# Later modulation columns: summed in the ticks of the attention instead of in the gated recurrence

## Chip, core and metric

The kernel runs on one core of a Trainium2 chip. The metric is device time in microseconds (us) of one execution, smaller is better. Three runs of the kernel before have a median of 3149.4 us.

## What is computed

One layer of a decoder trunk on 1024 tokens of width 1024, in float32. What matters for the change is where the modulation comes from and where it is used:

```
mod = silu(c) @ W_ada + b_ada -> sh1, sc1, g1, sh2, sc2, g2     # 6 x 1024 columns
h   = rms_norm(x) * (1 + sc1) + sh1
proj = h @ w_in                      # columns of three branches and of their gates
o_a = (rg_lru(conv4(lru_x)) * gelu(lru_y)) @ w_lru_o     # A: gated recurrence, width 1280
o_b = rwkv7_time_mix(...) @ w_rw_o                       # B: pairs of heads
o_c = sliding_window_attention(q, k, v) @ w_att_o        # C: 16 heads, 4 key heads, window 128
x   = x + g1 * ((gate_a * o_a + gate_b * o_b + gate_c * o_c) @ w_out)
h2  = rms_norm(x) * (1 + sc2) + sh2
x   = x + g2 * swiglu(h2)
```

The first 2048 columns of `mod` (sh1, sc1) are needed for h. The other 4096, here called the later columns, are first needed after the branches are merged.

## The kernel before, in words

Activations stand transposed: 128 channels on the partitions by 1024 tokens. Every dense product is made with operands split in a high and a low part, in three passes (`three_passes`, L246). One weight **block** is 1024 x 128 (512 KB): SP loads it into one of two slots of `w_raw` (`load_block`, L228; for the attention's keys and values in two halves, L546), POOL splits it into `w_hi` and `w_lo` (`split_block`, L236 and L238), and PE waits for the split before the block's first matmul and then runs 48 matmuls. A load waits until the block before the last is split, a split until the dense product before the last is done. Each engine executes its own list in order, and so does SP: a transfer behind a waiting one is not issued.

The stages stand one after the other: start, B in 8 turns, A in 2 turns, C, the merges of A, C and B, `w_out`, the feed-forward part.

**Gated recurrence (A), 2 turns of 5 column groups j.** PE's order in a turn is x0 x1 y0 x2 y1 x3 y2 x4 y3 y4 (`LRU_ORDER`), and after each y_j the eight matmuls of the gates (`lru_gates`, L866 and L867). They need the halo rows that ACT copies (L1204, L1206) once DVE has made the convolution of x_(j+1) (`conv`, one L1646 and three L1649), which needs ACT's copy of x_(j+1) out of PSUM (L1199). After the gates ACT takes sigmoids, exponentials and the root (L1211 to L1217), DVE makes the recurrence of group j (`recur`, L1668 to L1681), and ACT then waits for it and issues the store of `ya` to `y_a` (L1219), before it goes on. DVE's order is conv(j+1), sums of the later columns, recur(j).

**Later columns.** A product of a vector with a matrix: DVE multiplies weights with `c` on the partitions and adds up over 8 row tiles, and a matmul with a column of ones (L879) adds over the partitions. In a turn SP loads 16 blocks of 1024 rows by 128 columns in four lots of four (L538), each after the product two before it; DVE makes eight steps of 128x128 for each (`ada_sum`, L1421 and L1424), four blocks in each of the groups j = 0 to 3; PE sums four blocks at a time before y_1 to y_4, and waits for DVE there.

**Attention (C), 35 ticks.** A tick is a unit of two query blocks for a pair of heads; 8 ticks make a group with one key head. In tick t PE makes the scores of unit t (L952), transposes the probabilities of unit t - 2 (L965) and weighs the values of unit t - 3 (L977). Between these it puts 8 of the 48 steps of the next group's projection, in the first six ticks of a group: block 3 in ticks 0 and 1, block 4 in 2 and 3, block 5 in 4 and 5, block 6 in 8 and 9 and so on to block 11 in 20 and 21. Blocks 3, 6 and 9 hold keys and values. Ticks 6, 7, 14, 15 and all from 22 have no projection. DVE in tick t: `peaks(t)` (L1745 to L1754), `divide(t-1)` (L1760 to L1764), and in ticks 2, 3 and 6 of a group squares and norms of the next group (`k_sums` L1714 and L1717, `k_norm` L1722 and L1724, `q_rsqrt` L1731). SP's list there holds the blocks alone, then the first tiles of `y_a` (L561).

## Time and profile before

| | us |
|---|---|
| median of 3 runs | 3149.4 (3149.35 to 3154.89) |
| profiled execution: its own time | 3150.59 |
| profiled execution: span | 3148.8 |
| gated recurrence, 20 dense blocks | about 1289 to 1619 |
| attention's ticks | about 1671 to 1935 |

The profile's times are of one execution and count from the start of the span. Its page gives each engine's busy time and shares; the timeline lists instructions of one engine in order of time; the chain of waits is followed back from the last instruction. A row `x8` merges eight records; one float32 matmul that is no part of a split product leaves two records.

### The profile page before, as it was taken

To read this page: it belongs to the slowest core of one execution; us is meant where nothing else is said; L and a number is where in the kernel's file an instruction comes from. 1 tells how busy PE (TensorE), PEld (TensorE's weight loads), DVE (VectorE), ACT (ScalarE), POOL (GpSimd) and SP (SyncE) were. 2 spreads that over 40 slices of the span, in tenths; PEclk is the share of its full clock that TensorE was granted. 3 is DMA by queue.
4 is the path that set the end of the run, shared out by engine and by line. 5 is a ranking of instruction groups with operands and counts; after the bars stand their busy time and mean duration, and the time that the engine had idled before them with its cause. 6 is when DMAs were issued, how large, how long until landed. Compare 5 with 4: busy or idle time off the path is not lost.

```text
span 3148.8 us, 61688 instructions
## 1 busy us (share of the span) xinstructions
PE 2926.4 (93%) x25715; PEld 2385.0 (76%) x25715; DVE 1458.6 (46%) x1801; ACT 706.7 (22%) x1004; POOL 724.0 (23%) x454
## 2 busy tenths in 40 slices
PE   1899999999999999999979988989897999999998
PEld 1687878787888888776757766777685888888886
DVE  6555454555454554675744655445523222222222
ACT  1222121212121221244435664001202000000001
POOL 0212020203021111132312101333231333333331
PEclk7999999999999999999989998999897999999999
DMA  5111111102010110233421102333410111111111
GB/s 179 49 44 35 37 42 31 54 19 70 23 50 29 44 36 29 78 109 88 124 64 38 44 14 83 115 122 128 134 54 27 47 47 53 47 47 47 53 47 67
DMA packets 247066, 192.75 MB, mean 61 GB/s; under 512 B 21729, under 2 KB 225083, under 8 KB 246843
## 3 DMA queue, kind: packets, MB, share of 16 engines
q1 hardware_dynamic: 239136, 163.02, 17.5%
q10 hardware_dynamic: 7707, 26.34, 2.1%
q8 instruction: 191, 3.13, 0.4%
q14 instruction: 32, 0.26, 0.0%
HBM read 158.91 MB, written 30.41 MB: 60 GB/s over the span
## 4 chain that ended last, share of the span: by engine, by line
PE 84%; DVE 8%; ACT 4%; issue 3%; DMA 1%; ACTq 0%; DVEq 0%; POOL 0%; SPq 0%; POOLq 0%
PE ps L246 59%; PE ps L772 2%; PE ps L786 2%; PE ps L783 2%; PE ps L750 2%; DVE arena L1424 2%; PE ps L835 1%; PE ps L866 1%; PE ps L867 1%; PE ps L952 1%; PE ps L977 1%; PE ps L965 1%; DVE arena L1649 1%; PE ps L720 1%; ACT arena L1275 1%
## 5 line engine op out<-in xcount | busy, mean ns | idle before, releaser
L246 PE MATMUL ps<-x_hi,w_hi 128*128 128x512 f32 (+1 forms) x2576 | 839.5, 401 | 49.9 <-DVE x_lo L1850 17.7
L246 PE MATMUL ps<-x_lo,w_hi 128*128 128x512 f32 (+1 forms) x2576 | 821.8, 395 | 0.0
L246 PE MATMUL ps<-x_hi,w_lo 128*128 128x512 f32 (+1 forms) x2576 | 820.0, 394 | 0.0
L236 POOL CAST w_hi<-w_raw 128x1024 fp32r<-128x1024 f32 (+2 forms) x221 | 224.1, 1014 | 2365.4 <-PE ps L246 1629.4
L246 PEld LDWEIGHTS ps<-x_hi,w_hi 128*128 128x128 f32 (+1 forms) x2576 | 485.1, 191 | 189.6 <-issue 66.1
L246 PEld LDWEIGHTS ps<-x_hi,w_lo 128*128 128x128 f32 (+1 forms) x2576 | 489.6, 190 | 106.7
L246 PEld LDWEIGHTS ps<-x_lo,w_hi 128*128 128x128 f32 (+1 forms) x2576 | 490.9, 191 | 104.4
L238 POOL TENSOR_TENSOR w_lo<-w_raw,w_hi 128x1024 fp32r<-128x1024 f32 (+2 forms) x221 | 484.2, 2191 | 17.7
L1856 DVE TENSOR_TENSOR arena<-ps,arena 128x1024 f32<-128x1024 f32 x22 | 26.9, 1225 | 396.3 <-PE ps L246 396.3
L1873 DVE SCALAR_TENSOR_TENSOR arena<-ps,mod,arena 128x1024 f32<-128x1024 f32 x88 | 113.0, 1284 | 129.1 <-PE ps L246 129.1
L1591 DVE COPY_PREDICATED arena<-hid_lo,ps 128x256 f32<-128x256 int32 x144 | 72.0, 500 | 139.8 <-PE ps L783 90.4
L1424 DVE SCALAR_TENSOR_TENSOR arena<-arena,mod 128x128 f32<-128x128 f32 (+1 forms) x280 | 129.0, 461 | 10.0
L1374 ACT ACTIVATE hid_hi<-arena 128x1024 fp32r<-128x1024 f32 x22 | 23.4, 1062 | 450.7 <-PE ps L246 316.9
L246 PE MATMUL ps<-hid_hi,w_hi 128*128 128x512 f32 x352 | 109.1, 391 | 4.8 <-DVE hid_lo L1861 4.8
L246 PE MATMUL ps<-hid_lo,w_hi 128*128 128x512 f32 x352 | 108.8, 390 | 0.0
L246 PE MATMUL ps<-hid_hi,w_lo 128*128 128x512 f32 x352 | 108.8, 390 | 0.0
L1275 ACT ACTIVATE arena<-arena 128x256 f32<-128x256 f32 x128 | 75.4, 591 | 84.4 <-DVE arena L1754 84.4
L786 PE MATMUL ps<-arena 64*64 64x64 f32 x2560 | 89.4, 218 | 0.0
L1504 DVE TENSOR_TENSOR arena<-arena 128x1024 f32<-128x1024 f32 (+1 forms) x27 | 42.9, 1588 | 98.3 <-ACT arena L1120 97.3
L772 PE MATMUL ps<-arena 64*64 64x64 f32 x2560 | 84.5, 218 | 0.7
L786 PEld LDWEIGHTS ps<-arena 64*64 64x64 f32 x2560 | 83.2, 135 | 0.2 <-issue 0.2
L772 PEld LDWEIGHTS ps<-arena 64*64 64x64 f32 x2560 | 80.2, 135 | 1.7 <-issue 1.6
(263 smaller groups left out, 3541.5 us busy)
## 6 DMA issues: line engine op xcount, KB each, us to landing
w_raw<-in_w_in SPq DMA_DIRECT2D x78, 512.0 KB, 3.9
w_raw<-in_w_ffn_in SPq DMA_DIRECT2D x44, 512.0 KB, 3.8
arena<-in_w_ada SPq DMA_DIRECT2D x32, 512.0 KB, 3.8
gates_sig<-arena ACTq DMA_DIRECT2D x24, 512.0 KB, 2.6
arena<-gates_sig SPq DMA_DIRECT2D x24, 512.0 KB, 3.4
w_raw<-in_w_ffn_out SPq DMA_DIRECT2D x22, 512.0 KB, 3.5
arena<-in_x SPq DMA_DIRECT2D x16, 512.0 KB, 5.1
arena<-in_w_ada SPq DMA_DIRECT2D x8, 1024.0 KB, 12.0
```

Source lines behind the costliest of these rows:

```text
L236: nc.gpsimd.tensor_copy(hi, raw).then_inc(s_whi, 1)
L238: nc.gpsimd.tensor_tensor(lo, raw, hi.bitcast(F32), ALU.subtract).then_inc(s_wsplit, 1)
L246: ins = nc.tensor.matmul(dst[h], wp, xp[h], start=first and m == 0, stop=last and m == 2)
L750: ins = mm(dst, src[hp, c * CHUNK:(c + 1) * CHUNK], ar[hp, c, :, :], start=True, stop=True)
L772: ins = mm(bank(B, 2, hp)[:, c % BATCH, :], am[hp, c, AM_BA, :], xx[hp, 0, c, :], start=True, stop=True)
L783: ins = mm(bank(B, 0, hp)[:, c % BATCH, :], xx[hp, 1, c, :], y1[hp, c, :], start=True, stop=True)
L786: ins = mm(bank(B, 1, hp)[:, c % BATCH, :], y1[hp, c, :], xx[hp, 1, c, :], start=True, stop=True)
L1275: fn(sc[:, h, nn, :], sc[:, h, nn, :], ACT.Exp, bias=sm[:, SM_NEG, h, nn:nn + 1], scale=rq[:, gg % 2, t, n0 + nn, h:h + 1], accum_out=sm[: ...
L1424: ins = v.scalar_tensor_tensor(acc, w[:, k, :], c_k, acc, ALU.mult, ALU.add)
L1504: v.tensor_tensor(dst, x0, x1, ALU.subtract).then_inc(v_mix, 1)
L1591: v.copy_predicated(blocks_of(xx[:, o, batch(B), :], lv, o), level_mask(lv, o), blocks_of(bank(B, o), lv, o)).then_inc(v_xu, 1)
L1873: v.scalar_tensor_tensor(r, ps[:, 4 + 2 * (m % 2):6 + 2 * (m % 2), :], mod[:, MOD_G2 + m:MOD_G2 + m + 1], r, ALU.mult, ALU.add).then_inc(m ...
```

## The change

The 4096 later columns are taken 1024 columns by 128 rows a step: 32 steps, eight to each set of 1024 columns, 24 ticks. A step is one DVE instruction of 128x1024 (`later_ada`). The loads go through two free slots (`yraw`), each after the step two before it, and stand in SP's list between the blocks of the attention. PE sums each set with eight matmuls in ticks 6, 12, 18 and 24. One addition after the last tick puts the columns into `mod`, and PE waits for it before the merges. In the gated recurrence the loads, steps and sums go away; the store of group j is issued behind ACT's copy of x_(j+2), the last two behind the gelu and at the end. The load of the first tiles of `y_a` waits for all 32 steps.

```diff
         halo = lr["halo"].rearrange("p (s n) -> p s n", s=2)
...
         l_halo = made_by("act", "lru_halo_ready")
-        ada_acc1 = lr["acc"].rearrange("p (s m) -> p s m", s=4)
...
-        ADA_G = (LRU_G - 1) * ADA_PHASE
         s_adb = [sem(f"later_ada_weights_loaded_{k}") for k in range(2)]
...
-        l_pe, l_ada = made_by("pe", "lru_gates_done", "ada_sums_taken")
+        l_pe, t_ada = made_by("pe", "lru_gates_done", "later_ada_sums_taken")
         l_cv, l_sq, l_u, l_out, l_z, gw_zero = made_by(
...
-        mg = carve([("x2", KT * T), ("mix", KT * T), ("gt", 2 * T), ("t", 2 * T), ("pad", 1536), ("yraw", 2 * T)])
+        mg = carve([("x2", KT * T), ("mix", KT * T), ("gt", 2 * T), ("t", 2 * T), ("pad", 1536), ("yraw", 2 * T), ("more", T)])
...
         yraw = mg["yraw"].rearrange("p (s n) -> p s n", s=2)
+        ADA_TICKS = ALL - UNITS
+        ada_acc1 = mg["more"]
         gtl = mg["gt"].rearrange("p (s n) -> p s n", s=2)
...
                         load_gate_weights(g, j)
-                    if c in (4, 6, 8, 9):
-                        first = ADA_PHASE * (4, 6, 8, 9).index(c)
-                        for n in range(first, first + ADA_PHASE):
-                            sp.wait_ge(ada_acc, upto(g * ADA_G + (ADA0 + n - 1)))
-                            wait_alone(sp)
-                            sp.dma_start(ada_w1[:, n % 2, :, :], cols(w_ada, ADA0 * 256 + n * P + g * (ADA_G * P), P)).then_inc(s_adb[n % 2], 16)
+            def load_ada(first, last):
+                for n in range(first, last):
+                    sp.wait_ge(ada_acc, upto(ADA0 + n - 1))
+                    sp.dma_start(yraw[:, n % 2, :], w_ada[n % KT * P:(n % KT + 1) * P, 1024 * (n // KT + 2):1024 * (n // KT + 3)]).then_inc(s_adb[n % 2], 16)
...
                     sp.dma_start(dst[:, :, s, :], src).then_inc(s_w[b.slot] if s else s_kfirst, 16)
+                if gg > 0:
+                    load_ada(11 * (gg - 1), 11 * (gg - 1) + 3)
                 for t in range(2):
                     load_block(sp, Block("att", 3 * gg + 1 + t), cols(w_in, COL_Q + 256 * gg + P * t, P), P)
+                    if gg > 0:
+                        first = 11 * (gg - 1) + 3 * t + 3
+                        load_ada(first, min(first + 3 + 2 * t, ADA1))
                 if gg == 0:
...
                         sp.wait_ge(m_lo, upto(n - 1))
+                        sp.wait_ge(ada_acc, upto(ADA0 + ADA1))
                         sp.dma_start(yraw[:, n % 2, :], y[row0 + k * P:row0 + (k + 1) * P, :]).then_inc(s_y[n % 2], 16)
...
                 pe.wait_ge(v_post, upto(PAIRS * POST))
-                pe.wait_ge(ada_out, upto(g * (LRU_G - 1) + (ADA0 + j)))
                 n = 2 * 16 * len(PIECES_OF[j])
...
                         pe.wait_ge(a_gate, upto(PAIRS * 3))
-                    if kind == "y" and j > 0:
-                        pe.wait_ge(ada_acc, upto(g * ADA_G + (ADA0 + ADA_PHASE * j)))
-                        pe.wait_ge(l_sa, upto(g * (2 * LRU_G) + 2 * j))
-                        for q in range(ADA_PHASE):
-                            ins = mm(ps[:, 4, q:q + 1], ada_acc1[:, q, :], ones[:, 0:1], start=True, stop=True)
-                        ins.then_inc(l_ada, 1)
                     dense(pe, Block("lru", c, g))
...
                 ins.then_inc(t_o, 1)
+            def ada_sums(u):
+                pe.wait_ge(ada_acc, upto(ADA0 + KT * (u + 1)))
+                for n in range(8):
+                    ins = mm(ps[:, BANK_O, 256 + 8 * u + n:257 + 8 * u + n], ada_acc1[:, n * P:(n + 1) * P], ones[:, 0:1], start=True, stop=True)
+                ins.then_inc(t_ada, 1)
...
                     project(nx, fill + 3, fill + 6)
+                if 0 < tick <= ADA_TICKS and tick % 6 == 0:
+                    pe.wait_ge(t_oc, upto(tick - 3))
+                    ada_sums(tick // 6 - 1)
                 if 0 <= tick - 3 < ALL:
...
             pe.wait_ge(t_cp, upto(6 * GROUPS))
+            pe.wait_ge(ada_out, upto(ADA0 + 1))
             for g, (nm, kts, *_) in enumerate(BR):
...
             with act.Fori(0, TURNS["lru"]) as g:
+                def store_y(j):
+                    act.wait_ge(l_out, upto(g * LRU_G + (j + 1)))
+                    act.dma_start(y_a[bass.ds(g * (LRU_G * P) + j * P, P), :], lr["ya"]).then_inc(s_ya, 16)
                 for c, (kind, j) in enumerate(LRU_ORDER):
...
                         fn(halves(lr["xp"][:, 3:T + 3]), pair_of(blk.slot), ACT.Copy).then_inc(l_ev, 1)
+                        if j >= 2:
+                            store_y(j - 2)
                         continue
...
                     fn(halves(lr["gy"]), pair_of(blk.slot), ACT.Gelu_apprx_tanh).then_inc(l_ev, 1)
+                    if j == LRU_G - 1:
+                        store_y(j - 1)
                     act.wait_ge(l_pe, upto(g * LRU_G + (j + 1)))
...
                     fn(lr["a2"], lr["a2"], ACT.Sqrt, scale=-1.0, bias=one_b).then_inc(l_rt, 1)
-                    act.wait_ge(l_out, upto(g * LRU_G + (j + 1)))
-                    act.dma_start(y_a[bass.ds(g * (LRU_G * P) + j * P, P), :], lr["ya"]).then_inc(s_ya, 16)
+                    if j == LRU_G - 1:
+                        store_y(j)
...
-            def later_ada(g, j):
-                dve.wait_ge(l_ada, upto(g * (LRU_G - 1) + j))
-                for q in range(ADA_PHASE):
-                    n = ADA_PHASE * j + q
-                    dve.wait_ge(s_adb[n % 2], g * (16 * ADA_G // 2) + 16 * (n // 2 + 1))
-                    ada_sum(ada_acc1[:, q, :], ada_w1[:, n % 2, :, :], g * ((KT - 1) * ADA_G) + (KT - 1) * (ADA0 + n))
-            def later_ada_add(g, j):
-                dve.wait_ge(l_ada, upto(g * (LRU_G - 1) + (j + 1)))
-                cols4 = mod[:, bass.ds(g * ADA_G + (2 * ADA0 + ADA_PHASE * j), ADA_PHASE)]
-                v.tensor_tensor(cols4, ps[:, 4, 0:ADA_PHASE], cols4, ALU.add).then_inc(ada_out, 1)
+            def later_ada(n):
+                c_k = mod[:, 48 + n % KT:49 + n % KT]
+                dve.wait_ge(s_adb[n % 2], 16 * (n // 2 + 1))
+                if n % KT == 0:
+                    dve.wait_ge(t_ada, upto(n // KT))
+                    ins = v.tensor_scalar(ada_acc1, yraw[:, n % 2, :], c_k, None, ALU.mult)
+                else:
+                    dve.wait_ge(ada_acc, upto(ADA0 + n))
+                    ins = v.scalar_tensor_tensor(ada_acc1, yraw[:, n % 2, :], c_k, ada_acc1, ALU.mult, ALU.add)
+                ins.then_inc(ada_acc, 1)
...
                         conv(g, j + 1)
-                    if j > 0:
-                        later_ada_add(g, j - 1)
-                    if j + 1 < LRU_G:
-                        later_ada(g, j)
                     recur(g, j)
...
                     q_rsqrt(nx)
+                if tick < ADA_TICKS:
+                    for n in range(ADA1 * tick // ADA_TICKS, ADA1 * (tick + 1) // ADA_TICKS):
+                        later_ada(n)
                 if tick - 1 in Y_TICKS:
...
+            dve.wait_ge(t_ada, upto(ADA1 // KT))
+            dve.wait_ge(t_oc, upto(ALL))
+            later = mod[:, 2 * ADA0:2 * ADA0 + ADA1]
+            v.tensor_tensor(later, ps[:, BANK_O, 256:256 + ADA1], later, ALU.add).then_inc(ada_out, 1)
+            dve.wait_ge(ada_out, upto(ADA0 + 1))
             v.tensor_scalar(mod[:, MOD_SC2:MOD_SC2 + 8], mod[:, MOD_SC2:MOD_SC2 + 8], 1.0, None, ALU.add).then_inc(ada_fix, 1)
```

On **SP**, in the attention, the list of transfers (L546, after it L545, are halves of the keys' and values' block, L228 the others, L537 the later columns' weights). Before:

```order
L552 DMA arena<-in_consts 128x512
L546 DMA w_raw<-in_w_in 128x8x64 x2
L228 DMA w_raw<-in_w_in 128x8x128 x2
L546 DMA w_raw<-in_w_in 128x8x64 x2
L228 DMA w_raw<-in_w_in 128x8x128 x2
```

And with the change, the same stretch up to block 9:

```order
L556 DMA arena<-in_consts 128x512
L545 DMA w_raw<-in_w_in 128x8x64 x2
L537 DMA arena<-in_w_ada 128x1024 x3
L228 DMA w_raw<-in_w_in 128x8x128
L537 DMA arena<-in_w_ada 128x1024 x3
L228 DMA w_raw<-in_w_in 128x8x128
L537 DMA arena<-in_w_ada 128x1024 x5
L545 DMA w_raw<-in_w_in 128x8x64 x2
L537 DMA arena<-in_w_ada 128x1024 x3
L228 DMA w_raw<-in_w_in 128x8x128
L537 DMA arena<-in_w_ada 128x1024 x3
L228 DMA w_raw<-in_w_in 128x8x128
```

Every block from block 4 on stands behind a lot of three or five loads of the later columns.

On **ACT**, in the gated recurrence, around the copy of an x block. Before:

```order
L1217 ACTIVATE arena<-arena,bias_t 128x1024
L1219 ISA
L1219 DMA y_a<-arena 128x1024
L1196 REGISTER_ALU
L1199 ACTIVATE arena<-ps 128x1024
```

With the change (L1234 is L1217, L1212 is L1199, L1203 is L1219):

```order
L1234 ACTIVATE arena<-arena,bias_t 128x1024
L1209 REGISTER_ALU
L1212 ACTIVATE arena<-ps 128x1024
L1203 ISA
L1203 DMA y_a<-arena 128x1024
```

The copy now stands ahead of the store and of the wait for it.

On **DVE**, in tick 11 and the start of tick 12, with the change (L1735 is L1724, L1756 is L1745):

```order
L1733 RECIPROCAL arena<-arena 128x8
L1735 TENSOR_TENSOR arena<-arena 128x1024
L1677 SCALAR_TENSOR_TENSOR arena<-arena,mod 128x1024 x2
L1756 TENSOR_TENSOR arena<-ps,arena 128x1024
L1758 TENSOR_REDUCE arena<-arena 128x4
```

Before, L1745 followed L1724 at once; now two steps of the later columns stand between.

## Rows read from the trace of the kernel before


**Rows 1.** The page, busy time of each engine.

```profile
PE 2926.4 (93%) x25715; PEld 2385.0 (76%) x25715; DVE 1458.6 (46%) x1801; ACT 706.7 (22%) x1004; POOL 724.0 (23%) x454
```

**Rows 2.** Timeline of PE, recurrence: start us, us, line, form, [idle before <-releaser].

```profile
1329.02 1.12 PE L867 MATMUL ps<-arena 64*128 64x512 f32 x2
1330.07 0.72 PE L246 MATMUL ps<-x_hi,w_hi 128*128 128x512 f32 x2
...
1341.11 0.95 PE L879 MATMUL ps<-keep,arena 128*128 128x1 f32 x8
...
1354.57 1.12 PE L866 MATMUL ps<-arena 128*128 128x512 f32 x2 [1.48 <-ACT arena L1206]
...
1386.12 1.13 PE L866 MATMUL ps<-arena 128*128 128x512 f32 x2 [1.67 <-ACT arena L1206]
```

**Rows 3.** Timeline of PE, last y block of both turns.

```profile
1429.39 1.86 PE L879 MATMUL ps<-keep,arena 128*128 128x1 f32 x8 [4.58 <-DVE arena L1424]
...
1444.12 1.02 PE L866 MATMUL ps<-arena 128*128 128x512 f32 x2
...
1594.98 1.87 PE L879 MATMUL ps<-keep,arena 128*128 128x1 f32 x8 [6.61 <-DVE arena L1424]
...
1610.50 1.02 PE L866 MATMUL ps<-arena 128*128 128x512 f32 x2
```

**Rows 4.** Timeline of ACT, same stretch as rows 2.

```profile
1338.58 1.15 ACT L1217 ACTIVATE arena<-arena,bias_t 128x1024 f32<-128x1024 f32 x1
...
1345.92 1.03 ACT L1199 ACTIVATE arena<-ps 128x1024 f32<-128x1024 f32 x1 [6.19 <-DVE arena L1681]
...
1353.46 1.05 ACT L1206 ACTIVATE arena<-arena 64x1024 f32<-64x1024 f32 x1
```

**Rows 5.** Timeline of DVE, same stretch.

```profile
1343.53 1.69 DVE L1681 TENSOR_TENSOR arena<-arena 128x1024 f32<-128x1024 f32 x1 [0.22 <-DVE arena L1677]
1347.16 0.88 DVE L1646 TENSOR_SCALAR arena<-arena,lru_par 128x1024 f32<-128x1024 f32 x1 [1.93 <-ACT arena L1199]
...
1351.06 1.28 DVE L1649 SCALAR_TENSOR_TENSOR arena<-arena,lru_par 128x1024 f32<-128x1024 f32 x1 [0.15 <-DVE arena L1649]
```

**Rows 6.** Timeline of SP in attention: transfers issued.

```profile
1690.72 17.94 SPq L228 DMA_DIRECT2D w_raw<-in_w_in  x2
```

**Rows 7.** Tile w_raw, 1600 to 1800 us: ns min/median/max.

```profile
L236 POOL CAST w_hi<-w_raw x10: 1036/1036/1041, 1610.8 to 1791.6; 128x1024 fp32r<-128x1024 f32 x10
L238 POOL TENSOR_TENSOR w_lo<-w_raw,w_hi x10: 2342/2394/3247, 1611.9 to 1792.7; 128x1024 fp32r<-128x1024 f32 x10
```

**Rows 8.** DMA issues, 1313 to 1321 us: KB each, median us to landing.

```profile
arena<-in_w_ada SPq DMA_DIRECT2D x2, 512.0 KB, 4.6
```

**Rows 9.** Timeline of DVE in ticks 2, 6, 11 and 17.

```profile
1695.51 0.69 DVE L1717 TENSOR_REDUCE arena<-arena 128x8 f32<-128x512 f32 x1
...
1732.28 0.35 DVE L1731 RECIPROCAL arena<-arena 128x32 f32<-128x32 f32 x1 [4.28 <-ACT arena L1266]
...
1773.37 1.72 DVE L1724 TENSOR_TENSOR arena<-arena 128x1024 f32<-128x1024 f32 x1
...
1818.72 1.22 DVE L1764 TENSOR_TENSOR arena<-arena 128x1024 f32<-128x1024 f32 x1
```

**Rows 10.** The chain of waits in attention: start us, us, what.

```profile
1703.58 1.06 PE ps L952 x8
1704.64 2.27 PE ps L246 x9
...
1739.37 1.07 PE ps L965 x8
...
1772.70 1.06 PE ps L952 x8
...
1823.57 1.06 PE ps L952 x8
...
1877.57 1.94 PE ps L965 x8
```

6 lines of the change are left out of this document (2 added, 4 removed).

## Prediction

> **What bounds the kernel now.** I read the page first, then the chain of waits, then the timelines of the two stages that the change touches. PE is busy for 2926.4 of 3148.8 us [rows 1], so a gain must come from PE's 220 idle us or from work taken off PE, and whatever makes PE wait costs its full length. In the gated recurrence PE waits in two places. Before the gates of the middle blocks it waits 1.5 to 1.7 us for ACT's halo copy; one period lasts 1386.12 - 1354.57 = 31.55 us [rows 2]. Before the last y block of each turn it waits 4.58 and 6.61 us for DVE's sums of the later columns [rows 3]. In the attention's ticks with a projection PE is back to back: scores at 1703.58, projection at 1704.64 without a gap [rows 10].
>
> **The recurrence.** Removed: 256 small DVE instructions, 32 loads, 8 lots of four matmuls, and the waits on them.
>
> *Middle blocks.* What PE waits for is a chain: DVE finishes `ya` at 1343.53 + 1.69 = 1345.2, ACT, which had stood at the store since its root ended at 1339.7, copies x (1345.92), DVE starts the convolution at 1347.16, ends it at 1352.3, ACT ends the second halo at 1354.5, PE starts the gates at 1354.57 [rows 2, 4, 5]. With the store behind the copy, the copy is done long before 1345.2, and the convolution starts about 0.1 us after `ya`: at 1345.3, 1.85 us earlier. PE would be there at 1353.1 less 0.8 for the four matmuls that go, 1352.3, against 1352.7 for the halo: the gain is 1.85. Three periods in each of two turns: 6 x 1.85 = **11.1 us**.
>
> *Last y block.* The gates before it end at 1429.39 - 4.58 = 1424.81. A dense block takes 1341.11 - 1330.07 = 11.04 [rows 2], so the next gates could start at 1435.85 instead of 1444.12: 8.3 us. ACT's halo is ready then too: it has no store in front any more and ends its root 9.5 us after the gates (1339.7 against 1330.1), the halo 1.1 later. In the second turn 1594.98 - 6.61 + 11.04 = 1599.41 instead of 1610.50: 11.1 us [rows 3]. Together **19.4**. The stage gains 30.5.
>
> **The attention: SP's list.** Here I expect the loss. Count steps p0 to p31 and loads n0 to n31. DVE makes steps 32t/24 up to 32(t+1)/24 (rounded down) in tick t; load n waits for step p(n-2). By the list, block 4 stands behind n2 (waits for p0, tick 0), block 5 behind n5 (p3, tick 2), block 6 behind n10 (p8, tick 6), block 7 behind n13 (p11, tick 8), block 8 behind n16 (p14, tick 11), block 9 behind n21 (p19, tick 14), block 10 behind n24 (p22, tick 17), block 11 behind n27 (p25, tick 19). PE needs them in ticks 2, 4, 8, 10, 12, 16, 18 and 20. Now such a block leaves when its slot is free, far ahead: blocks 7 and 8 at 1690.72 and 1708.3, in ticks 2 and 4 [rows 6].
>
> *From a finished step to a split block:* SP wakes 0.1, issues the later columns' load 0.5, the block lands 5.0 after its issue (two such loads together take 4.6 at the median, the second is the later one [rows 8]), POOL wakes 0.1 and splits in 1.04 + 0.1 + 2.39 [rows 7]: **9.2 us**; 9.7 for a block in two halves.
>
> *A step* of 128x1024 out of SBUF takes 1.3 us as the convolution's does (1.28), the first of a set 0.9 (L1646) [rows 5].
>
> - Block 5: p3 ends at 1695.51 + 0.69 + 2 x 1.3 = 1698.8, the block is ready at 1708.0, needed at 1704.64 [rows 9, 10]: 3.4.
> - Block 6: p8 stands behind the root at 1732.28 + 0.35, ends at 1733.5, ready at 1743.2. PE makes 2.27 us of projection and then transposes, today at 1739.37: 1743.2 + 2.3 - 1739.4 = 6.1.
> - Block 8: p14 stands behind `k_norm`, 1773.37 + 1.72, ends at 1776.4, ready at 1785.6, needed at 1772.70 + 1.06: 11.8.
> - Block 9: as block 6, but two full steps, 1.8 later: 7.9.
> - Block 10: p22 ends at 1818.72 + 1.22 + 1.3 = 1821.2, ready at 1830.4, needed at 1823.57 + 1.06: 5.8.
> - Block 11: as block 8, with a `k_norm` 0.5 shorter: 11.3.
> - Blocks 4 and 7 are ready about one and about six us before they are needed.
>
> Sum **46.3 us** of PE waiting.
>
> *Clock.* After the waits of 4.58 and 6.61 us the matmuls run slow: from the four small matmuls to the gates the two turns take 14.73 and 15.52 us [rows 3], in the middle blocks 1354.57 - 1.48 - 1341.11 = 11.98 [rows 2]. So such a wait costs 2.75 to 3.5 us more; waits of 1.5 to 1.7 do not. Block 5's wait (3.4) is nearest to the 4.58, the other five are as long or longer: 2.75 + 5 x 3.15 = **18.5**.
>
> *Small terms.* PE's eight-matmul sums: 0.95 for four [rows 2], so 1.7; in tick 6 hidden behind ACT, in ticks 12 and 18 on PE's path: 3.4. In ticks 22 to 24 DVE and ACT set the pace: p29 puts 1.3 ahead of the next `peaks`, and the sum of tick 24 runs at the slow clock that the transposition there shows (1.94 [rows 10] against 1.07), 1.87 for four [rows 3], 3.5: together 4.8. The addition before the merges: 0.3. The steps in other ticks lie in DVE's gaps: about 4.7 us of its work in ticks of 9.3. If that cover were gone, each step would cost 1.3.
>
> **Sum:** -30.5 + 46.3 + 18.5 + 3.4 + 4.8 + 0.3 = +42.8. The profiled execution took 3150.6, 1.2 above the median of 3149.4; on the median's side **3192 us**.
>
> Bounds: a block that lands in 3.9 would be ready 1.1 earlier (-6.6 in six); landing one us later and L238's slowest 3.25 give +11. The clock's term lies between 0 and 6 x 3.5 = 21. The recurrence may gain 26 to 33. That is 3149.4 + 15 = 3164 to 3149.4 + 60 = 3209.
>
> A rule to weigh. Two loads issued together landed in 4.6 us [rows 8]. The Trainium skill, "DMA: Bandwidth & Descriptors", section on the anatomy of one DMA, gives for loads issued by GpSimd a fixed 2 us plus the bytes at 436 GB/s: an estimate of 4.4 us for two of 512 KB from the first one's issue, where I count 5.5. By it the six waits would be 6.6 us shorter and the time 3185. The same page of the Trainium skill, section "Issuing engines are not separate DMA queues", says that spreading transfers over issuing engines saves only issue time; by that the place of a load in SP's list would be nearly free. It is not what I argue, since a wait in that list holds back everything behind it; no run here shows it yet.
>
> **Rivals.**
> 1. *The clock holds.* The PE work in the ticks is of smaller matmuls, and the slow stretch might be shorter or absent. For: the transposition at 1739.37 follows a wait for ACT and takes 1.07, not 1.94 [rows 10]. Against: the two long waits of [rows 3]. 42.8 - 18.5 gives 3174. Chance 0.17.
> 2. *The blocks come in time*, faster than before: if products ran ahead of the ticks, or blocks could leave without them, PE would never wait for a split. It decides at block 8: its load must leave 11.8 us earlier, before tick 11's `peaks`. For: DVE is busy only 46% of the span [rows 1]. Against: the list. Then -30.5 + 8.5 = -22: 3127. Chance 0.07.
> 3. *DVE becomes a bound as well*: steps wait for their own loads (which stand behind blocks in the same list), `peaks` comes late and ticks 4 to 21 stretch: one step, 1.3 us, in 15 more ticks gives 20 on top, 3212. Chance 0.13.
> 4. *The gain and the loss cancel*: the waits overlap with others of PE and only half remains: within 0.2%. Chance 0.03.
>
> My case has 0.60. About 0.2% is what a measurement of this kernel can tell from no change. **Faster** by more than that: 0.07; **the same** 0.03; **slower** 0.90. The range reaches from the case's lower end, which takes in rival 1, to its upper one, where rival 3 begins: 3163 to 3209.
>
> **What would show it.** In the changed profile: the list of PE's waits names POOL's w_lo some six times, longest in ticks 12 and 20 (about 12 us each); SP waits for DVE's steps; POOL waits for the transfer of `w_raw`; L866's wait for ACT falls under 0.5 us and periods to 29.7; the wait before the last y block is gone, the recurrence ends 30 us earlier. The matmuls after each wait run at half speed for some us. I am wrong if PE does not wait for splits in the ticks, if the stage before gives less than 25 us, or if DVE is what PE waits for there.

## The result, and the profile after

| | kernel before | changed kernel |
|---|---|---|
| median of 5 runs | 3154.2 us (3149.4 to 3156.9) | 3217.0 us (3211.6 to 3230.4) |
| ratio | 1 | 1.0216 (1.0185 to 1.0247) |
| profiled execution, span | 3148.8 us | 3228.6 us |

The change makes the kernel slower by 2.2%; 3217 us lies above the range of the forecast (3163 to 3209). A second set of runs of the changed kernel (run 6, further down) gives 1.0170 (1.0142 to 1.0199). I read the time stage by stage first, from the starts of four landmarks on PE: the first gates, the last gates, the first scores, and the start of the merges.

| profile | before | after | difference | predicted |
|---|---|---|---|---|
| start to first gates (no line of it changed) | 1321.7 | 1344.3 | +22.5 | 0 |
| first gates to last gates (recurrence) | 288.8 | 273.8 | -15.0 | -30.5 |
| last gates to first scores | 60.5 | 60.7 | +0.2 | 0 |
| first scores to merges (attention) | 263.9 | 334.6 | +70.7 | +73.3 |
| merges to the end | 1213.8 | 1215.2 | +1.4 | 0 |

So the attention lost what was foreseen, the recurrence gave half of what was foreseen, and 22.5 us stand in a stage that nothing touches. Three questions follow, and the experiments take them in that order.

The page of the changed kernel, busy times, answers to [rows 1]. PE has the same number of matmul records and is busy 33 us longer, so some of them ran slower:

```profile
PE 2959.7 (92%) x25715; PEld 2403.1 (74%) x25715; DVE 1411.3 (44%) x1570; ACT 708.4 (22%) x1004; POOL 731.2 (23%) x454
```

The list of waits of PE, then of SP (engine, tile and line, what it waited for: us in total, times, longest us). The first line is the one that grew: in the kernel before it stands at 1.3 us, once, and not in the attention. Six of the seven waits now are in the ticks. At L870 the wait for ACT's halo, which was to go, is 15.2 us in six (9.7 in six before):

```profile
PE ps L246 <- POOL w_lo L238: 52.0, 7, 12.2
...
PE ps L870 <- ACT arena L1221: 15.2, 6, 2.6
```

```profile
SPq L537 <- DVE arena L1677: 197.1, 26, 18.9
...
SPq L537 <- DVE arena L1674: 87.1, 4, 37.7
```

**Attention.** The six waits in the ticks, from PE's timeline, in the order of blocks 5, 6, 8, 9, 10 and 11:

```profile
1718.47 0.80 PE L246 MATMUL ps<-x_hi,w_hi 128*128 128x512 f32 x1 [5.08 <-POOL w_lo L238]
...
1758.37 0.80 PE L246 MATMUL ps<-x_hi,w_hi 128*128 128x512 f32 x1 [4.92 <-POOL w_lo L238]
...
1808.50 0.79 PE L246 MATMUL ps<-x_hi,w_hi 128*128 128x512 f32 x1 [11.54 <-POOL w_lo L238]
...
1854.75 0.80 PE L246 MATMUL ps<-x_hi,w_hi 128*128 128x512 f32 x1 [7.93 <-POOL w_lo L238]
...
1882.43 0.79 PE L246 MATMUL ps<-x_hi,w_hi 128*128 128x512 f32 x1 [7.72 <-POOL w_lo L238]
...
1916.03 0.80 PE L246 MATMUL ps<-x_hi,w_hi 128*128 128x512 f32 x1 [12.16 <-POOL w_lo L238]
```

They sum to 49.35 us; the forecast had 3.4, 6.1, 11.8, 7.9, 5.8 and 11.3, together 46.3. The longest chain but one, block 8, row by row from the timelines of DVE, SP and POOL:

```profile
1796.80 1.23 DVE L1735 TENSOR_TENSOR arena<-arena 128x1024 f32<-128x1024 f32 x1
1797.94 2.67 DVE L1677 SCALAR_TENSOR_TENSOR arena<-arena,mod 128x1024 f32<-128x1024 f32 x2
```

```profile
1799.69 0.38 SPq L228 DMA_DIRECT2D w_raw<-in_w_in  x1
```

```profile
1804.79 1.24 POOL L236 CAST w_hi<-w_raw 128x1024 fp32r<-128x1024 f32 x1 [30.71 <-DMA w_raw<-in_w_in]
1806.11 2.34 POOL L238 TENSOR_TENSOR w_lo<-w_raw,w_hi 128x1024 fp32r<-128x1024 f32 x1
```

Step p14 is the first of the two, behind `k_norm`; it ends at about 1799.3 (half of 2.67 on top of 1797.94). The block leaves at 1799.69, POOL has it at 1804.79 and has split it at 1808.45: 9.2 us from the step to the split, as reckoned. From the block's issue to the start of its split it is 5.1 us, as counted (5.0 and 0.1). POOL had stood 30.7 us without work, and the slot was free all that time.

**Recurrence.** The last y block of each turn gained as foreseen: its gates come 17.9 us behind the ones before instead of 26.4 and 29.3, together 19.9 us (19.4 predicted). The middle blocks gained nothing. Their gates on PE's timeline answer to the L866 rows of [rows 2]:

```profile
1377.07 1.22 PE L870 MATMUL ps<-arena 128*128 128x512 f32 x1 [2.40 <-ACT arena L1221]
```

The next gates start at 1410.26 and 1443.48 behind waits of 2.62: periods of 33.2 us where I had forecast 29.7 and [rows 2] show 31.55. (The first period of a turn is 1.3 us longer than the others in both kernels, 32.8; the same holds in the runs below.) The timelines of ACT, POOL and DVE in one such period:

```profile
1363.83 1.03 ACT L1212 ACTIVATE arena<-ps 128x1024 f32<-128x1024 f32 x1 [1.57 <-PE ps L246]
...
1367.91 0.34 ACTq L1203 DMA_DIRECT2D y_a<-arena  x1
...
1374.88 1.06 ACT L1219 ACTIVATE arena<-arena 64x1024 f32<-64x1024 f32 x1 [10.02 <-DVE arena L1666]
```

```profile
1363.95 2.72 POOL L236 CAST w_hi<-w_raw 128x1024 fp32r<-128x1024 f32 x1 [15.90 <-PE ps L246]
...
1366.75 3.25 POOL L238 TENSOR_TENSOR w_lo<-w_raw,w_hi 128x1024 fp32r<-128x1024 f32 x1
```

```profile
1363.54 2.29 DVE L1692 TENSOR_TENSOR_SCAN arena<-arena 128x1024 f32<-128x1024 f32 x1
...
1366.06 1.69 DVE L1696 TENSOR_TENSOR arena<-arena 128x1024 f32<-128x1024 f32 x1 [0.23 <-DVE arena L1692]
...
1367.67 2.88 DVE L1663 TENSOR_SCALAR arena<-arena,lru_par 128x1024 f32<-128x1024 f32 x1
...
1370.69 1.28 DVE L1666 SCALAR_TENSOR_TENSOR arena<-arena,lru_par 128x1024 f32<-128x1024 f32 x1
```

ACT's x copy (L1212) is out of the way at 1364.9, and the convolution's first step L1663 starts right behind `ya` (L1696), all as forecast. But that step, 0.88 us in [rows 5], now lasts 2.88. It ends at 1370.55, and POOL's L238 ends at 1370.00. Now the kernel before, POOL in the same stretch as [rows 5]:

```profile
1341.43 2.72 POOL L236 CAST w_hi<-w_raw 128x1024 fp32r<-128x1024 f32 x1 [15.91 <-PE ps L246]
1344.23 3.25 POOL L238 TENSOR_TENSOR w_lo<-w_raw,w_hi 128x1024 fp32r<-128x1024 f32 x1
```

L238 ends at 1347.48, and the first step of [rows 5] at 1347.16 + 0.88 = 1348.04: 0.56 us later, as in the changed kernel (0.55). From POOL's start to PE's gates it is 13.14 us before (1354.57 - 1341.43) and 13.12 after. The two engines seem to take turns: scan, cast, `ya`, subtraction, first step, each ending just after the other has let go, with 2.72 for a cast that takes 1.04 alone and 3.25 for a subtraction of 2.34. The trace of the kernel before already shows such steps some 30 us ahead of [rows 5], at the start of the turn: a later step of the first x block beside POOL's subtraction of 1304.72 to 1307.97, and the first step of the second x block beside that of 1312.30 to 1314.69, which ends 0.54 us before the step does:

```profile
1305.88 3.17 DVE L1649 SCALAR_TENSOR_TENSOR arena<-arena,lru_par 128x1024 f32<-128x1024 f32 x1 [0.17 <-DVE arena L1649]
...
1312.40 2.83 DVE L1646 TENSOR_SCALAR arena<-arena,lru_par 128x1024 f32<-128x1024 f32 x1 [1.92 <-ACT arena L1199]
```

No store of `y_a` is issued there, which speaks against a store as the cause.

**Theory C** is that DVE and POOL share a way into SBUF and that the split, which PE releases at the same moment as the x copy, was a second chain as long as the one that I had read. **Rival D** is that the store's transfer, issued at 1367.91, stretches the step.

### The profile page after: what moved, and what is told of

Same layout as the page of the kernel before. It is cut to its first block, busy times and chain, and to the rows that moved or that the text cites. A ratio compares the mean times of both kernels' runs of the same rounds, so it can differ in the third digit from the quotient of the medians.

```text
span 3228.6 us, 61109 instructions
## 1 busy us (share of the span) xinstructions
PE 2959.7 (92%) x25715; PEld 2403.1 (74%) x25715; DVE 1411.3 (44%) x1570; ACT 708.4 (22%) x1004; POOL 731.2 (23%) x454
## 4 chain that ended last, share of the span: by engine, by line
PE 82%; DVE 8%; ACT 4%; issue 3%; DMA 2%; POOL 1%; ACTq 0%; DVEq 0%; SPq 0%; POOLq 0%
PE ps L246 57%; PE ps L777 2%; PE ps L791 2%; PE ps L788 2%; PE ps L755 2%; PE ps L870 1%; PE ps L871 1%; PE ps L840 1%; DMA w_raw<-in_w_in 1%; DVE arena L1441 1%; PE ps L725 1%; PE ps L724 1%; ACT arena L1292 1%; DVE arena L1666 1%; PE ps L950 1%
## 5 line engine op out<-in xcount | busy, mean ns | idle before, releaser
L238 POOL TENSOR_TENSOR w_lo<-w_raw,w_hi 128x1024 fp32r<-128x1024 f32 (+2 forms) x221 | 487.7, 2207 | 17.7
L1875 DVE TENSOR_TENSOR arena<-ps,arena 128x1024 f32<-128x1024 f32 x22 | 26.9, 1225 | 394.7 <-PE ps L246 394.7
L1391 ACT ACTIVATE hid_hi<-arena 128x1024 fp32r<-128x1024 f32 x22 | 23.4, 1063 | 450.4 <-PE ps L246 316.9
L1576 DVE TENSOR_TENSOR arena<-ps,arena 128x1024 f32<-128x1024 f32 x8 | 9.8, 1224 | 176.0 <-PE ps L699 176.0
```

What stands on the lines that cost most here:

```text
L238: nc.gpsimd.tensor_tensor(lo, raw, hi.bitcast(F32), ALU.subtract).then_inc(s_wsplit, 1)
```

## Experiments

All were timed beside runs of the kernel before on the same chip. Its median there was 3159 to 3163 us, so ratios are what can be compared. The last table of this section has the stage lengths of every profile. Code is cut; `...` marks what is left out.

**1. Blocks first in SP's list** (attention; theory A against B).

```
+            LOTS = {3: (0, 2), 6: (2, 5), 7: (5, 8), 8: (8, 11), 9: (11, 16), 10: (16, 19), 11: (19, ADA1)}
...
-                if gg > 0:
-                    load_ada(11 * (gg - 1), 11 * (gg - 1) + 3)
+                load_ada(*LOTS.get(3 * gg, (0, 0)))
...
-                    if gg > 0:
-                        first = 11 * (gg - 1) + 3 * t + 3
-                        load_ada(first, min(first + 3 + 2 * t, ADA1))
+                    load_ada(*LOTS.get(3 * gg + 1 + t, (0, 0)))
```

`LOTS` names the block behind which a lot of loads stands, and its first and last load.

> The changed kernel, with SP's list in the attention merged by time: each weight block stands where its slot comes free, and the loads of the later columns are put behind it (block 7 behind three loads that wait, not behind twelve). Nothing else differs. Theory A (the blocks stand behind loads that wait for DVE's steps): PE's 52 us of waits for POOL's split in the ticks fall under 3 us, the attention from the first scores to the merges goes from 334.6 to about 265 us (52 of waits and 18 of slow clock behind them), and the time from 3217 to about 3147. Rival B (DVE's steps or the 16.8 MB of extra loads are what stretches the ticks): the attention stays over 300 us and the time over 3180. If only the waits go and the clock stays slow: 3165.

Measured: 3157.6 us, ratio 0.9994 (0.9972 to 1.0017). The list of PE's waits in that profile has one wait for a split left, the one outside the attention that the kernel before has too:

```profile
PE ps L246 <- POOL w_lo L238: 1.3, 1, 1.3
```

SP waits for DVE's steps as before, only nothing stands behind:

```profile
SPq L539 <- DVE arena L1676: 165.9, 26, 13.7
```

The attention takes 276.0 us, 58.6 less, and with it goes nearly all of the loss. Theory A holds, B falls: the same 32 loads and 32 steps are there. 58.6 is 49.4 of waits and 9 of what is left for the clock; I had put the clock at 18.5. (In the profile of run 6 it is 57.2 in all, 48.2 of waits and again 9. In the first profile 4 of the 9 lie in ticks 22 to 31, behind the last wait for a split, so 9 is rather an upper bound there.)

What stays above the kernel before is 12.1 us against its first profile (276.0 against 263.9) and 10.4 and 9.3 against its two others, runs 10 and 11; my small terms came to 8.5. From the first scores to those of tick 22 run 1 takes 201.5 us, against 189.4, 192.3 and 192.2; from there to the merges 74.5, against 74.5, 73.3 and 74.5. The starts of the scores give each tick. Ticks 5, 9 to 11, 13, 17 and 19 to 21 hold steps and are as long as before within 0.1 us, so there the steps are hidden, as I had said. Longer than in runs 10 and 11 are tick 4 (1.8, a wait of 1.6 for `k_norm`), tick 6 (3.5), ticks 12 and 18 (2.5 and 1.6), and ticks 7, 15 and 16 (4 together); ticks 8 and 14 are shorter by 4. Ticks 6, 12 and 18 are those with PE's sums of eight matmuls, which take 1.84 us:

```profile
1841.56 1.84 PE L981 MATMUL ps<-keep,arena 128*128 128x1 f32 x16
```

I had put 3.4 for ticks 12 and 18, nothing for tick 6 and 4.8 for the ticks from 22 on, where the whole costs nothing.

**2. The late store alone, on the kernel before** (C against my reading of the chain).

```
                         fn(halves(lr["xp"][:, 3:T + 3]), pair_of(blk.slot), ACT.Copy).then_inc(l_ev, 1)
+                        if j >= 2:
+                            store_y(j - 2)
...
                     fn(lr["a2"], lr["a2"], ACT.Sqrt, scale=-1.0, bias=one_b).then_inc(l_rt, 1)
-                    act.wait_ge(l_out, upto(g * LRU_G + (j + 1)))
-                    act.dma_start(y_a[bass.ds(g * (LRU_G * P) + j * P, P), :], lr["ya"]).then_inc(s_ya, 16)
```

> The kernel before, with nothing changed but the place of y_a's store on ACT (behind the next x copy). What I predicted of this part: the convolution starts 1.85 us earlier in six periods, periods of 29.7 us instead of 31.55, time 11 us less, 3143. Theory C (the convolution's first step can't end before POOL's split of the next block has ended, since both want the same way into SBUF): the first step starts earlier and lasts longer (about 2.9 us instead of 0.88), ends at the same moment, 0.55 us behind the end of POOL's second instruction, and the time stays at 3154 within 3 us.

Measured: 3158.8 us, ratio 1.0002 (0.9980 to 1.0023). The periods are 31.57 and 31.55 us, PE's wait for the halo 1.48 to 1.69 as before. The convolution's first step now starts at 1343.74, beside POOL's subtraction, and lasts 2.88 us, in all six middle blocks, as theory C has it. The recurrence is 283.5 us, and 283.8 and 283.6 in the two further profiles of the kernel before (runs 10 and 11). The late store by itself is worth nothing on this kernel: this is the 11.1 us term of the forecast, and it is zero.

**3. POOL's split waits for the convolution** (C against D), on the changed kernel.

```
-        def split_block(pool, blk, n):
+        def split_block(pool, blk, n, also=None):
...
+            if also is not None:
+                pool.wait_ge(l_cv, also)
...
-                        split_block(pool, Block(name, c, i), n)
+                        split_block(pool, Block(name, c, i), n,
+                                    upto(i * (4 * LRU_G) + 2 * (c + 1)) if name == "lru" and c in (3, 5, 7, 9) else None)
```

> The changed kernel, with one more wait on POOL: in the recurrence the split that would start with the x copy (blocks 3, 5, 7 and 9 of a turn) waits until DVE has done the convolution. Theory C (DVE's scan, its ya and its first step of the convolution alternate with POOL's two instructions, one at a time): the first step takes 0.9 us instead of 2.88 and ya 1.2 instead of 1.69, the convolution ends 2.3 us earlier, PE's wait before the gates of the middle blocks falls from 2.4 us to under 0.5, periods from 33.2 to 30 to 31 us: 14 to 22 us less in all, 3195 to 3203. Rival D (what stretches the first step is y_a's store, which ACT issues at the same moment): the step still takes 2.9 us, and the time stays at 3217 or gets worse. PE does not wait for the later split: it is done some 8 us before the gates end.

Measured: 3196.2 us, ratio 1.0115 (1.0077 to 1.0153). DVE's and PE's timelines in a middle block:

```profile
1382.88 1.23 DVE L1699 TENSOR_TENSOR arena<-arena 128x1024 f32<-128x1024 f32 x1 [0.21 <-DVE arena L1695]
1384.02 0.81 DVE L1666 TENSOR_SCALAR arena<-arena,lru_par 128x1024 f32<-128x1024 f32 x1
```

```profile
1391.35 1.13 PE L873 MATMUL ps<-arena 128*128 128x512 f32 x2
```

`ya` takes 1.23 instead of 1.69, the first step 0.81 instead of 2.88 with the store's transfer issued at 1384.27, beside it. PE waits under 0.1 us, the periods are 28.98 us (30.27 for the first of a turn), and the recurrence is 253.5 instead of 273.8: -20.3. C holds, D falls.

**4. Both edits together.**

> The changed kernel with both edits (blocks first in SP's list, POOL's split behind the convolution). They touch different stages, so by A and C the gains add: 3217 - 70 - 18 = about 3129, 25 us faster than the kernel before. If A holds and C does not: 3147. If they don't add, one of them was paid for with clock speed of the stage behind it.

Measured: 3145.6 us, ratio 0.9949 (0.9926 to 0.9972). Recurrence 253.4, attention 276.5: the two add, and this is faster than both kernels. The expectation was too good: it had 25 us under the kernel before, and the ratio says 16 (9 to 23). It had counted the attention back at 265 us, and, as in run 1, some 10 us stay.

**5. POOL's wait alone, on the kernel before.**

> The kernel before with POOL's split behind the convolution, and nothing else: the sums of the later columns stay in the recurrence and y_a's store stays ahead of the x copy. Together with the store alone (0 us in the middle blocks) and both together (33.2 to 28.98 us a period) it tells whether the two gains add or mask each other. If they mask (theory C): the chain is then again ya, store, x copy, convolution, as I had read it; ya ends 0.45 us earlier, the first step still starts behind the x copy, periods go from 31.55 to about 30.9, and the time is 4 us less than the kernel before (3158 beside 3162). If they just add: 2.3 us a period, 14 us less. The wait before the last y block stays at 4.6 and 6.6 us.

Measured: 3175.0 us, ratio 1.0033 (1.0015 to 1.0051): slower, which neither number of mine allowed. `ya` is short (1.22), and the first wait before the middle gates of a turn falls to 0.94. The second rises to 2.3 and 2.5, and DVE's next work behind the convolution, its sums of the later columns, shows why:

```profile
1372.33 7.03 DVE L1427 SCALAR_TENSOR_TENSOR arena<-arena,mod 128x128 f32<-128x128 f32 x6
...
1379.59 2.68 DVE L1427 SCALAR_TENSOR_TENSOR arena<-arena,mod 128x128 f32<-128x128 f32 x7
```

Seven such instructions take 2.68 us; six take 7.03 when POOL's two splits run beside them (L238 and L240 there, from 1371.0 to 1378.1). In the kernel before the first seven take 5.37, since one split of the two runs there already (1353.25 to 1356.83). The recurrence step that follows starts 16.2 us behind the gates (1389.26 - 1373.10), and 13.5 in the kernel before (1368.05 - 1354.57). The collision moves from the convolution to the sums, so the periods are 32.2 to 32.7 us. It took the removal of the sums, which leaves DVE 15.5 to 17.1 us idle in a period (run 3 and the changed kernel), to make a place for the split. The recurrence of 292.0 us is 3.2 to 8.4 above the three profiles of the kernel before; the ratio says 5 to 16 us for the whole.

**6. The changed kernel again.**

> The changed kernel once more, with nothing edited, beside the same runs of the kernel before as the others. The RWKV turns of the profiles so far last either about 143 or about 148 us whatever the kernel: theory E says that this is chance of the granted clock, not the change's. Then this profile shows another mix of the two lengths, the recurrence again takes 272 to 274 us and the attention 332 to 334 us from scores to the last values, and the ratio of the medians is 1.017 to 1.019 (3150 + 57 over 3150), under the first one's 1.0216. If the change does slow the RWKV turns, most of its seven turns last 147 us or more again and the ratio stays at 1.021 or over.

Measured: 3222.6 us, ratio 1.0170 (1.0142 to 1.0199). Recurrence 275.4, attention 333.2. The ratio is in the range that theory E gave. But six of the seven turns of the RWKV stage (the stage ahead of the recurrence) last over 147 us, which was the sign of the other side, so this run alone did not decide; runs 10 and 11 bear on it.

**7. The first step reads PSUM** instead of ACT's copy, on the changed kernel.

```
-v.tensor_scalar(xa, xpv[:, 3:3 + T], lp(...), lp(LP_CB), ALU.mult, ALU.add)
+v.tensor_scalar(halves(xa), pair_of(Block("lru", LRU_AT["x", j], g).slot), lp(...), lp(LP_CB), ALU.mult, ALU.add)
```

With it, PE waits before the third block of a turn until this step has read the first block, which it would otherwise overwrite.

> The changed kernel with the convolution's first step reading the block straight out of PSUM instead of ACT's copy in SBUF; the three steps behind it still read two inputs in SBUF. It tells which steps have to wait for POOL. Theory C1 (every step with a second reader in SBUF waits): the first step takes 1.1 to 1.3 us beside POOL's L238, the second one is stretched to its end (to about 2 us), the convolution ends 0.7 us earlier, PE's wait goes from 2.4 to 1.7 us: 4 to 6 us in all. C2 (only the fast first form waits): it ends 1.8 us earlier, 11 us in all. Rival D (the store's transfer stretches whatever DVE does): the first step is as long as before, no gain.

Measured: 3209.7 us, ratio 1.0130 (1.0097 to 1.0164). DVE's and POOL's timelines:

```profile
1391.58 1.33 DVE L1665 TENSOR_SCALAR arena<-ps,lru_par 128x1024 f32<-128x1024 f32 x1
1393.05 4.81 DVE L1668 SCALAR_TENSOR_TENSOR arena<-arena,lru_par 128x1024 f32<-128x1024 f32 x3
```

```profile
1390.66 3.26 POOL L238 TENSOR_TENSOR w_lo<-w_raw,w_hi 128x1024 fp32r<-128x1024 f32 x1
```

The step from PSUM runs through POOL's L238 in 1.33 us, and takes 1.34 at 1475.84, where POOL does nothing. The three behind it, with both inputs in SBUF, take 4.81 together, 4.14 in run 3; L238 ends at 1393.92, 0.9 us into the first of them. PE's wait is 1.5 to 1.7 us, as C1 says. The recurrence is 263.7, 10 us less: more than C1's 4 to 6 and near C2's 11, but not by C2's way. The convolution ends 0.9 us earlier and the periods are 30.63, where the changed kernel has 31.53 at full clock; the rest is the clock, which fell behind three of its six waits of 2.4 to 2.6 us (periods of 33.2) and behind none here.

Of this the Trainium skill, "SBUF — State Buffer", section "Who interferes with whom", says that DVE and GpSimd share one pair of SBUF ports, that a DVE instruction in its fast two-port form contends with GpSimd, the first one in holding the pair for its whole length and the other fully blocking, and that one with two SBUF inputs contends with a GpSimd instruction that reads SBUF. The trace agrees: 2.88 us against 0.81 for the first step out of SBUF (taken to be the fast form, since it does in 0.81 what takes 1.34 out of PSUM), 4.81 against 4.14 for three steps with two inputs, and no stretch for the step out of PSUM.

**8. Steps placed** clear of `k_sums` and `k_norm`, on top of run 4.

```
+        ADA_STEPS = (0, 1, 4, 5, 6, 7, 8, 9, 12, 13, 14, 15, 16, 17, 20, 21)
+        ADA_SUMS = (6, 10, 16, 22)
...
+            LOTS = {3: (0, 2), 6: (2, 6), 8: (6, 10), 9: (10, 18), 11: (18, ADA1)}
...
+                if tick in ADA_STEPS:
+                    for n in range(2):
+                        later_ada(2 * ADA_STEPS.index(tick) + n)
```

> The kernel with both edits (blocks first, split behind the convolution), with DVE's steps two at a time in the ticks without k_sums and k_norm (0, 1, 4 to 9, 12 to 17, 20, 21), the sums on PE in ticks 6, 10, 16 and 22, and the loads ordered for that. The attention took 274.4 us from scores to last values with both edits and 262.4 in the kernel before; if the 12 us between come from steps that delay k_norm (PE's 1.6 us wait for it in tick 4, slower ticks 4, 12 and 19), some 5 of them go: 269 us, and about 3140 for the whole. If they come from the sums on PE and from DVE's load as such, it stays at 274; if pairs of steps delay the peaks, it grows.

Measured: 3136.0 us, ratio 0.9905 (0.9874 to 0.9937): the fastest of the study, some 30 us under the kernel before. The attention is 270.4 us from scores to last values. But the wait of 1.6 us in tick 4, on which the expectation hung part of the gain, is still there:

```profile
PE ps L927 <- DVE arena L1738: 1.6, 1, 1.6
```

So the size came out and the reason did not. The stretches from the first scores to those of tick 22, and from there to the merges, in run 4 and then in run 8 (the first figure behind the window is its length):

```profile
1651.27:1852.70 201.43, 196.11 (x1235) 152.52 (x1234) 139.97 (x217) 116.20 (x288) 24.77 (x14) 0.94 0.33 99
1852.70:1927.80 75.10, 53.40 (x433) 43.09 (x433) 56.03 (x93) 48.72 (x125) 3.71 (x4) 0.82 0.26 87
...
1650.99:1852.90 201.91, 197.00 (x1233) 153.37 (x1232) 145.18 (x220) 116.17 (x288) 25.58 (x14) 0.94 0.34 102
1852.90:1923.60 70.70, 51.21 (x434) 40.69 (x433) 51.79 (x90) 48.75 (x125) 3.70 (x4) 0.86 0.24 82
```

Up to tick 21 nothing is gained; tick 4 takes 11.1 us in both. Ticks 12 and 18, which lost PE's sum, are 2.5 and 1.7 us shorter, and ticks 10 and 16, which got it, 1.6 and 2.6 longer: most of that price goes with the sum. Steps ahead of `k_norm` are not what makes tick 4 long, since run 8 has none in ticks 2 and 3. The 4.4 us come from tick 22 on, where run 8 has no steps and one sum. Which of the two gave them was not tried.

**9. The old store on top of run 8.**

> The kernel of the placed steps (blocks first, POOL's split behind the convolution) with y_a's store back at its old place, ahead of the x copy and of the halo. It prices the late store where POOL is out of the way. By my reading of the chain ya, store, x copy, convolution: the convolution starts 1.8 us later in six periods, which go from 28.98 to 30.8 us (11 in all), and each turn's last gates wait for ya and the store, 23.4 us behind the gates before instead of 17.9 (11 in all): the recurrence goes from 253.4 to 275, up to 10 more if the clock falls behind the waits, the time from 3136 to 3158 to 3168. If the late store is worth nothing here either: 253 and 3136.

Measured: 3181.6 us, ratio 1.0069 (1.0042 to 1.0095). Against run 8 that is 52 us by the ratios, more than the 22 to 32 expected. The edit puts the store back ahead of the copy and of the halo. The periods are 30.97 us instead of 28.98: 2.0 us each, where the forecast had 1.85 for this chain (one of the six is 32.67). With POOL out of the way my term is right. The last gates of both turns come 23.9 us behind the ones before (23.4 expected). What was not expected is what follows; PE's timeline and the stretches behind that wait (us of the stretch, busy time of each engine with its instructions, then the granted clock):

```profile
1447.47 2.08 PE L873 MATMUL ps<-arena 128*128 128x512 f32 x2 [5.88 <-ACT arena L1222]
```

```profile
1447.00:1450.00 3.00, 2.52 (x3) 1.00 (x4) 0.00 (x0) 2.73 (x3) 0.96 (x1) 0.50 0.34 139
1450.00:1455.00 5.00, 5.00 (x6) 1.00 (x4) 0.00 (x0) 0.00 (x0) 0.00 (x0) 0.50 0.00 0
1455.00:1460.00 5.00, 5.00 (x6) 1.50 (x6) 0.00 (x0) 0.00 (x0) 0.00 (x0) 0.50 0.00 0
...
1463.00:1468.00 5.00, 5.00 (x15) 3.63 (x15) 0.00 (x0) 4.21 (x4) 0.00 (x0) 0.67 0.10 18
```

The clock stands at 0.50 (1.2 GHz) for the whole set of gates and on to 1466.3, 18.8 us of work without a gap, and a matmul pair takes 2.08 us instead of 1.13. To the next turn's gates it is 50.1 us instead of 41.2, and from the last gates to the scores 68.2 instead of 60.6: 8.9 and 7.6 us for the two waits, beyond the waits themselves. Of the 52 us the profiles show 43: 34.6 in the recurrence, 7.6 up to the scores and 0.8 in the attention.

**10 and 11. The kernel before, unedited** (theory E).

> The kernel before with nothing edited, for the lengths of its RWKV turns. Theory E (each turn lasts about 143 or about 148 us by chance of the granted clock, in any kernel): some two to six of the seven turns last over 146 us, another mix than in the first profile (two), and this stage lasts between 1320 and 1345 us; all that follows is as before within 2 us (recurrence 289, attention 262.4, the rest 1214). If the turns of this kernel are always short, as in its first profile, the change itself slows this stage, and the first gates stand at 1322 us again.

> The same once more: by theory E again another mix of long and short turns, first gates between 1320 and 1345 us and not at the same time as in the other two profiles of this kernel.

Measured: 3149.8 and 3157.1 us, first gates at 1327.0 and 1331.4 us. The recurrence is 283.8 and 283.6 us, and not within 2 us of 289 as expected, so the first profile was a costly one there too. One turn of the RWKV stage lasts from one store of y_b to the next. The first profile of the kernel before has 148.1, 143.3, 143.7, 143.3, 145.0, 148.3, 142.4; run 10 has 148.2, 144.0, 143.2, 143.3, 143.2, 144.2, 147.1; run 11 has 144.0, 143.3, 145.2, 148.7, 144.3, 148.1, 149.5. The first two turns of the first of these, as stretches with the granted clock behind POOL's busy time, and then the same piece of each of the two turns in close-up:

```profile
282.26:430.32 148.06, 144.42 (x2194) 121.85 (x2193) 74.26 (x90) 30.37 (x38) 25.03 (x13) 0.97 0.13 39
430.32:573.58 143.26, 139.56 (x2194) 119.99 (x2193) 74.24 (x90) 30.37 (x38) 25.02 (x13) 1.00 0.13 40
...
312.40:322.60 10.20, 10.20 (x16) 4.26 (x15) 9.16 (x8) 1.02 (x1) 2.86 (x1) 0.50 0.19 51
...
460.46:470.66 10.20, 10.20 (x37) 6.38 (x36) 9.12 (x8) 1.03 (x1) 2.83 (x1) 1.00 0.18 51
```

The same 2194 matmuls take 4.9 us longer at 0.97 than at 1.00, and the 0.97 is one stretch of 10.2 us at 0.50 (1.2 GHz). It begins 30 us into the turn, and PE is busy without a gap there and before; just before it come 64 small matmuls (L715), as they do in the turn that keeps its clock. So it is in all thirteen profiles: each of the 52 turns over 146 us has one such stretch of 6.8 to 13.7 us that begins 30 to 32.5 us into it, and none of the 39 shorter turns has one. So the same kernel draws its turns anew in each execution. What tips them was not found. It stays open whether the change shifts the odds.

| profile | turns over 146 us, of 7 | first gates | recurrence | attention (scores to last values) | span |
|---|---|---|---|---|---|
| before | 2 | 1321.7 | 288.8 | 262.4 | 3148.8 |
| run 10, before | 2 | 1327.0 | 283.8 | 264.0 | 3148.0 |
| run 11, before | 3 | 1331.4 | 283.6 | 265.1 | 3155.2 |
| run 2, late store only | 2 | 1320.3 | 283.5 | 264.2 | 3140.8 |
| run 5, split waits, on before | 4 | 1340.8 | 292.0 | 264.1 | 3169.8 |
| after | 7 | 1344.3 | 273.8 | 332.4 | 3228.6 |
| run 6, after again | 6 | 1346.1 | 275.4 | 331.1 | 3228.1 |
| run 1, blocks first | 5 | 1339.2 | 272.1 | 273.8 | 3161.3 |
| run 3, split waits | 4 | 1332.1 | 253.5 | 333.6 | 3194.4 |
| run 7, first step from PSUM | 4 | 1337.5 | 263.7 | 330.2 | 3207.2 |
| run 4, both | 5 | 1337.2 | 253.4 | 274.4 | 3140.6 |
| run 8, steps placed | 4 | 1337.0 | 253.4 | 270.4 | 3139.6 |
| run 9, old store | 4 | 1329.4 | 288.0 | 271.2 | 3171.0 |

The profiles by themselves suggest that it does: kernels that come from the kernel before have 13 long turns of 35 and their first gates at 1328 us on the average, those that come from the changed one 39 of 56 and 1338. The timed runs speak against that. From the first gates to the end, the eight profiles of kernels that come from the changed one differ from the mean of the three of the kernel before by 60.3 (after), 58.0 (run 6), -1.9, 38.3, 45.7, -20.6, -21.4 and 17.6 us (runs 1, 3, 7, 4, 8 and 9); the ratios of the timed runs, turned into us, give 68, 54, -2, 36, 41, -16, -30 and 22. The mean of the differences between the two rows is -0.4 us, so on the average the timed runs leave nothing for a slower first stage. The profiled executions differ from the timed ones in just this: those of the kernel before and of runs 2 and 5 took 2 to 16 us less than the median of their timed runs, while the eight others lie 9 us under to 13 over theirs; on the average the two groups are 9 us apart in this, about what their first gates are apart (10). That the change leaves the first stage alone is thus likely, and not proved: a single set of timed runs is uncertain by 7 to 12 us.

## Why the prediction was wrong

The direction and the mechanism of the loss were right, the size was not: 3192 forecast, 3217 measured. By its steps:

- **SP's list, 46.3 us: right.** 49.4 measured in the six blocks named, the largest miss 1.9 us (block 10), the way from step to split 9.2 us as reckoned. Run 1 shows the cause: with the blocks ahead of the waiting loads the waits are gone, with nothing else changed.
- **The clock behind the waits, 18.5 us: twice too much.** The changed kernel and run 1 leave 9 us for it at most. I took 2.75 to 3.5 us a wait from two waits in front of the gates [rows 3]; in runs 10 and 11 the first of these is 3.67 us long and costs 1.5. In the ticks the matmuls were slow for 6 us after a wait of 11.5 us (1808.5 to 1814.4) and then full again.
- **Small terms, 8.5 us: right in size, in part in the wrong place.** Run 1 has 9 to 12, all of it before tick 22: PE's sums in ticks 12 and 18 as counted (4.1 for 3.4), tick 6, which I had as hidden, 3.5, and 1.8 in tick 4; from tick 22 on nothing, where I had 4.8.
- **The last y blocks, 19.4 us: right for the profile shown** (19.9), but that profile had the most costly recurrence of three: 288.8, where runs 10 and 11 have 283.8 and 283.6. Against these the changed recurrence of 273.8 to 275.4 is worth only 8 to 10 us.
- **The middle blocks, 11.1 us: this step failed.** "What PE waits for is a chain", I wrote, with ACT's store and copy in it. The rows [rows 4, 5] were in order of time and touched, so I took them for the cause. A second chain, PE's dense block, POOL's cast and subtraction, and the convolution's first step, ended at the same moment; I had POOL's 3247 ns in [rows 7] as the slowest of ten and read it as scatter, not as a collision, and did not look at the first step of 2.83 us beside it that the trace of the kernel before already had. Run 2 gives 0 us for the late store, and after the change PE even waits 2.4 to 2.6 us instead of 1.5 to 1.7, because it comes 0.8 us earlier, without the four small matmuls, to the same end of the chain; behind such a wait three of the four later periods ran at a slow clock for some us and lasted 33.2 us instead of 31.5: +4.9 us instead of -11.1. Runs 3 and 9 show that the 1.85 us a period were a right price for a chain that did not bind: with POOL's split moved it is 2.0. My own sign for this was that the stage gives less than 25 us; it gave 15.
- **The base.** The three runs I had gave 3149.4; with two more the median was 3154.2, so that 5 of the 25 us missed are the base, and 3159 to 3163 in the later sets. In the profiles the forecast misses by 37 us (+79.8 against +42.8): 15.5 are the recurrence, -2.6 the attention, and 22.5 the first stage, which in the profiles of the unedited kernel alone differs by 10 us.

That the attention's 73.3 came so near to the 70.7 is in part luck: against the first profile the waits and the small terms were too small by 3 and 4 us, and the clock's term too large by 9.

Of the rivals, none was the case. DVE never became what PE waits for in the ticks for long: its scores wait 4.6 us for it in two waits. The rule that I weighed, from the Trainium skill, "DMA: Bandwidth & Descriptors", section "Issuing engines are not separate DMA queues", says that issuing transfers on several engines saves only the time to issue them; I had read from it that the place of a load in SP's list would be nearly free. Run 1 does not agree with that use of it: the place alone is worth 58.6 us of attention, since in these traces a load that waits holds all behind it in SP's list.

## What to carry to other kernels

When a wait seems explained by the rows just before it, look for a second chain released by the same event that ends at the same time: an instruction that lasts three times its usual length or ends each time at the same distance from another engine's end, is one. A load that waits for a computation belongs behind every load that could leave now, and one more run of the kernel before is worth having before a difference of under 1% is put down to an edit.
